# Folded norm sums, an activation scaled on ScalarE, and a layer norm joined with its modulation, in a two-block transformer kernel

## The reference, cut to what matters

```
# first block, end of each half (y: projected result, T x 1024)
x  = x + gate * rms_norm(y, g)              # after gla_out and after ffn_out
h2 = rms_norm(x, g') * (1 + scale) + shift  # input of ffn_in
# second block
h3 = x * (1 + scale_a) + shift_a            # input of qkv (no norm)
x  = layer_norm(ALPHA * x + gate_a * mix, ln1_g, ln1_b)
h4 = x * (1 + scale_f) + shift_f            # input of up
out = layer_norm(ALPHA * x + gate_f * down, ln2_g, ln2_b)
```

## Time and profile before

| | |
|---|---|
| median of 3 runs | 1060.26 us (1060.14 to 1066.72) |
| profiled execution | 1059.05 us, span 1057.3 us |
| PE busy | 980.9 us (93%) |
| DVE busy | 703.9 us (67%) |
| ACT busy | 551.0 us (52%) |
| norm sums on PE (line 614) | 112 instructions, 31.1 us |
| DMA | 196.79 MB, mean 186 GB/s |

### The profile page before, as it was taken

How to read it: one execution, slowest core, us unless ns; L and a number is a source line. 1 busy time by engine, 2 the same in 40 slices (tenths; PEclk the granted TensorE clock), 3 DMA queues, 4 the chain that set the end, 5 groups by cost and what they waited for, 6 DMA issues and landing times.

```text
span 1057.3 us, 19933 instructions
## 1 busy us (share of the span) xinstructions
PE 980.9 (93%) x8478; PEld 918.5 (87%) x8478; DVE 703.9 (67%) x1098; ACT 551.0 (52%) x830; POOL 27.2 (3%) x70
## 2 busy tenths in 40 slices
PE   5897999979999999699999999989999699999996
PEld 1477999869999999599898999888898699999995
DVE  2669937547777766598865543555668578888743
ACT  2658431555544443565745342656764466666433
POOL 2010000000000000130100000000000000000000
PEclk9898999999999999899999999999999989999999
DMA  9632765536888888247433436444357525555931
GB/s 329 234 121 80 264 234 187 181 127 212 278 275 283 281 274 309 72 149 252 153 120 102 149 113 169 140 160 132 110 201 228 208 99 184 189 188 188 331 100 40
DMA packets 57113, 196.79 MB, mean 186 GB/s; under 512 B 6064, under 2 KB 10560, under 8 KB 56768
## 3 DMA queue, kind: packets, MB, share of 16 engines
q1 hardware_dynamic: 51552, 187.72, 52.3%
q10 hardware_dynamic: 5216, 7.53, 2.6%
q0 software_dynamic: 256, 0.26, 0.1%
HBM read 194.43 MB, written 1.06 MB: 185 GB/s over the span
## 4 chain that ended last, share of the span: by engine, by line
PE 81%; DVE 9%; ACT 5%; DMA 3%; issue 1%; SPq 0%; ACTq 0%; DVEq 0%
PE panel_banks L401 67%; DMA raw<-in_panels 3%; PE work_banks L786 2%; DVE w_lo L1478 2%; PE work_banks L614 2%; ACT w_hi L969 1%; PE work_banks L573 1%; DVE raw L1511 1%; PE work_banks L715 1%; PE panel_banks L454 1%; PE work_banks L757 1%; PE work_banks L546 1%; PE work_banks L869 1%; PE work_banks L488 1%; PE work_banks L814 1%
## 5 line engine op out<-in xcount | busy, mean ns | idle before, releaser
L401 PE MATMUL panel_banks<-act_hi,w_hi 128*128 128x256 f32 (+1 forms) x1600 | 463.3, 290 | 26.3 <-DVE act_lo L1674 11.4
L401 PE MATMUL panel_banks<-act_lo,w_hi 128*128 128x256 f32 (+1 forms) x1600 | 454.5, 284 | 0.0
L401 PE MATMUL panel_banks<-act_hi,w_lo 128*128 128x256 f32 (+1 forms) x1600 | 453.9, 284 | 0.0
L1478 DVE TENSOR_TENSOR w_lo<-raw,w_hi 128x1024 fp32r<-128x1024 f32 x260 | 315.3, 1222 | 163.5 <-ACT w_hi L969 162.8
L969 ACT ACTIVATE w_hi<-raw 128x1024 fp32r<-128x1024 f32 x260 | 272.0, 1054 | 151.4 <-PE panel_banks L401 130.4
L401 PEld LDWEIGHTS panel_banks<-act_hi,w_hi 128*128 128x128 f32 x1600 | 304.6, 190 | 39.5 <-issue 19.5
L401 PEld LDWEIGHTS panel_banks<-act_lo,w_hi 128*128 128x128 f32 x1600 | 304.7, 190 | 1.8 <-issue 0.5
L401 PEld LDWEIGHTS panel_banks<-act_hi,w_lo 128*128 128x128 f32 x1600 | 304.4, 190 | 1.4
L401 PE MATMUL panel_banks<-hidden_hi,w_hi 128*128 128x256 f32 x352 | 98.0, 278 | 2.3 <-ACT hidden_hi L1186 2.3
L401 PE MATMUL panel_banks<-hidden_hi,w_lo 128*128 128x256 f32 x352 | 97.9, 278 | 0.0
L401 PE MATMUL panel_banks<-hidden_lo,w_hi 128*128 128x256 f32 x352 | 97.7, 278 | 0.0
(11 more groups left out here) (269 smaller groups left out, 1032.9 us busy)
## 6 DMA issues: line engine op xcount, KB each, us to landing
raw<-in_panels SPq DMA_DIRECT2D x356, 512.0 KB, 5.0
mix_work<-delta_rows ACTq DMA_DIRECT2D x2, 1024.0 KB, 11.8
x_t<-in_x ACTq DMA_DIRECT2D x1, 1024.0 KB, 9.4
gla_work<-in_ctx_x ACTq DMA_DIRECT2D x1, 1024.0 KB, 14.3
mix_work<-in_rel_bias ACTq DMA_DIRECT2D x1, 1024.0 KB, 10.0
out_x<-ffn_work SPq DMA_DIRECT2D x2, 512.0 KB, 2.6
mix_work<-in_rel_bias ACTq DMA_DIRECT2D x1, 768.0 KB, 14.3
c_wide<-in_c_rows ACTq DMA_DIRECT2D x1, 512.0 KB, 16.6
```

Of the source, the lines that this page charges most:

```text
L401: ins = pe.matmul(out_, a, b, start=start and p == 0, stop=stop and p == 2, skip_group_check=True)
L1478: dve.tensor_tensor(wlo[:, v_ % PARTS, :], raw[:, u % RAW, :], whi[:, v_ % PARTS, :].bitcast(F32), ALU.subtract)\
```

## The change: what it does

Five edits. (1) DVE adds the squares of two tiles (`fold`), so PE sums four tiles in place of eight, in the norm after `gla_out`, the one after `ffn_out`, and both variances; for the layer norm's mean DVE adds the two residual tiles into `sq2`. (2) After `ffn_out` ACT's last two weight copies, and DVE's subtractions for them, come behind the squares. (3) h3 is scaled on ACT instead of DVE. (4) The first layer norm's gain and bias are multiplied with the modulation on 128x8 columns, and h4 comes straight from `y3`; the plain result `xt` is made during turns 4 to 13 of the up projection, one tile a turn on DVE and then ACT. (5) The output is stored two tiles at a time.

```diff
-            for k in (0, 4):
+            for k in (0, 2, 4, 6):
...
-            def norm_part(name, count, r, src, bank=0, signal="norm_sum"):
+            def norm_part(name, count, r, src, bank=0, signal="norm_sum", tiles=1):
                 pe.wait_ge(S(name), count + r + 1)
-                for k in (2 * r, 2 * r + 1):
+                for k in range(2 * r, 2 * r + tiles):
...
             for i in range(11):          # ACT, ffn_out (DVE's loop likewise)
-                upper_parts(j + 2)
+                if i < 10:
+                    upper_parts(j + 2)
...
+            upper_parts(j + 1)           # ACT, after the four pairs
             act.wait_ge(S("norm_sum"), 4)
             factor(rs[:, 0:T], MB[:, 0, 0:T], D, 0, "norm_factor")
-            upper_tiles("h3_ready", lambda k: h3[:, k, :], "h3_hi")
+            for r in range(4):
+                act.wait_ge(S("x_new"), 5 + r)
+                for k in (2 * r, 2 * r + 1):
+                    act.activation(h3[:, k, :], xt[:, k, :], ACT.Identity, scale=..., bias=...)
+                for k in (2 * r, 2 * r + 1):
+                    act.wait_ge(S("h3_ready"), k + 1)
+                    act.activation(hhi[:, k, :], h3[:, k, :], ACT.Copy).then_inc(S("h3_hi"), 1)
...
+            def fold(wait_for, count, name):
+                dve.wait_ge(S(wait_for), count)
+                r = (count - 1) % 4
+                dve.tensor_tensor(sq2[:, 2 * r, :], sq2[:, 2 * r, :], sq2[:, 2 * r + 1, :], ALU.add).then_inc(S(name), 1)
+            for i in range(4):           # DVE, gla_out
+                fold("squares", i + 1, "folded")
+                if i < 3:
+                    lower_parts(j + 2)
+                j += 1
...
+            for r in range(4):           # DVE, after ffn_out
+                fold("squares", 9 + r, "folded")
+            lower_parts(j + 1)
+            for r in range(5):
+                if r < 4:
+                    normed(4, r)
+                    add_normed(r)
+                if r:
+                    for k in (2 * r - 2, 2 * r - 1):
+                        lower_tile(k, h3[:, k, :], "h3")
...
             def residual(turn, r):
-                dve.scalar_tensor_tensor(group(y3, r), group(xt, r), ALPHA, group(y3, r), ALU.mult, ALU.add)\
-                    .then_inc(S("ln_in"), 1)
+                then(dve.scalar_tensor_tensor(group(y3, r), group(xt, r), ALPHA, group(y3, r), ALU.mult, ALU.add))
+                dve.tensor_tensor(sq2[:, 2 * r, :], y3[:, 2 * r, :], y3[:, 2 * r + 1, :], ALU.add).then_inc(S("ln_in"), 1)
...
                 for r in range(4):       # DVE, layer_norm
                     dve.tensor_tensor(group(y3, r), group(y3, r), over_tiles(rs[:, 0:T], 2), ALU.subtract)
+                    if r >= 2:
+                        fold("ln_squares", 4 * count + r - 5, "folded")
+                for r in (2, 3):
+                    fold("ln_squares", 4 * count + r - 3, "folded")
...
+            dve.tensor_tensor(gcol[:], sc_a[:, 1, :], col("ln1_g_2", 0, 8), ALU.mult)
+            then(dve.tensor_tensor(sc_a[:, 0, :], sc_a[:, 1, :], col("ln1_b_2", 0, 8), ALU.mult))
+            then(dve.tensor_tensor(sc_a[:, 0, :], sc_a[:, 0, :], mod2[:, 24:32], ALU.add))
+            layer_norm(1)
+            staggered(lambda k: dve.scalar_tensor_tensor(h2[:, k, :], y3[:, k, :], gcol[:, k:k + 1], rs[:, T:2 * T],
+                                                         ALU.mult, ALU.mult).then_inc(S("ln_scaled"), 1),
+                      lambda k: lower_tile(k, h2[:, k, :], "h4", bias=sc_a[:, 0, k:k + 1]))
...
+                if 4 <= i < 4 + KT:      # DVE, in the up projection, before lower_parts
+                    dve.scalar_tensor_tensor(y3[:, i - 4, :], y3[:, i - 4, :], col("ln1_g_2", i - 4), rs[:, T:2 * T], ...)
...
+                if 6 <= i < 6 + KT:      # ACT, in the up projection, before the wait for up_done
+                    act.wait_ge(S("ln_scaled"), KT + i - 5)
+                    act.activation(xt[:, i - 6, :], y3[:, i - 6, :], ACT.Identity, bias=col("ln1_b_2", i - 6))
```

More of the change, by code:

```diff
@@ L299, in _ @@
                     .then_inc(S(f"landed{u % RAW}"), 16)
-            for k in (0, 4):
-                sp.wait_ge(S("out_ready"), k + 4)
-                sp.dma_start(out[:, k:k + 4], f_out[:, k:k + 4]).then_inc(S("out_stored"), 16)
-            sp.wait_ge(S("out_stored"), 32)
+            for k in (0, 2, 4, 6):
+                sp.wait_ge(S("out_ready"), k + 2)
+                sp.dma_start(out[:, k:k + 2], f_out[:, k:k + 2]).then_inc(S("out_stored"), 16)
+            sp.wait_ge(S("out_stored"), 64)
         @block.gpsimd
@@ L608, in _ @@
             gla_norm(3)
-            def norm_part(name, count, r, src, bank=0, signal="norm_sum"):
+            def norm_part(name, count, r, src, bank=0, signal="norm_sum", tiles=1):
                 pe.wait_ge(S(name), count + r + 1)
-                for k in (2 * r, 2 * r + 1):
+                for k in range(2 * r, 2 * r + tiles):
                     ins = pe.matmul(MB[:, bank, 0:T], ones[:, 0:P], src[:, k, :], start=(k == 0),
-                                    stop=(k == KT - 1))
+                                    stop=(k == 6 + tiles - 1))
                 if r == 3:
@@ L628, in _ @@
                 else:
-                    norm_part("squares", 0, n - 1, sq2)
-            norm_part("squares", 0, 3, sq2)
+                    norm_part("folded", 0, n - 1, sq2)
+            norm_part("folded", 0, 3, sq2)
             for r in range(4):
@@ L634, in _ @@
                     pe.wait_ge(S("norm_factor"), 2)
-                norm_part("squares", 4, r, sq2)
+                norm_part("squares", 4, r, sq2, tiles=2)
             for i in range(22):
@@ L687, in _ @@
             for r in range(4):
-                norm_part("squares", 8, r, sq2)
+                norm_part("folded", 4, r, sq2)
             for i in range(12):
@@ L1217, in _ @@
                 ins.then_inc(S("panel_evacuated"), 1)
+            upper_parts(j + 1)
             act.wait_ge(S("norm_sum"), 4)
             factor(rs[:, 0:T], MB[:, 0, 0:T], D, 0, "norm_factor")
-            upper_tiles("h3_ready", lambda k: h3[:, k, :], "h3_hi")
+            for r in range(4):
+                act.wait_ge(S("x_new"), 5 + r)
+                for k in (2 * r, 2 * r + 1):
+                    act.activation(h3[:, k, :], xt[:, k, :], ACT.Identity, scale=sc_a[:, 1, k:k + 1], bias=mod2[:, k:k + 1])\
+                        .then_inc(S("h3_ready"), 1)
+                for k in (2 * r, 2 * r + 1):
+                    act.wait_ge(S("h3_ready"), k + 1)
+                    act.activation(hhi[:, k, :], h3[:, k, :], ACT.Copy).then_inc(S("h3_hi"), 1)
             def delta_rows():
@@ L1405, in _, with layer_norm @@
                 j += 1
[L1407 removed]
+            def layer_norm(count):
                 act.wait_ge(S("ln_sum"), count)
@@ L1415, in layer_norm @@
                 factor(rs[:, T:2 * T], MB[:, 1, 0:T], D, 1, "ln_factor")
[L1416 to L1429, removed]
+            layer_norm(1)
+            upper_tiles("ln_scaled", lambda k: h2[:, k, :], "h4_hi", bias=lambda k: sc_a[:, 0, k:k + 1])
             for i in range(22):
@@ L1440, in _ @@
                     hidden_upper(i - 1, "hidden2_gated")
+                if 6 <= i < 6 + KT:
+                    act.wait_ge(S("ln_scaled"), KT + i - 5)
+                    act.activation(xt[:, i - 6, :], y3[:, i - 6, :], ACT.Identity, bias=col("ln1_b_2", i - 6))\
+                        .then_inc(S("x3_ready"), 1)
                 act.wait_ge(S("up_done"), i + 1)
@@ L1457, in _ @@
                 ins.then_inc(S("panel_evacuated"), 1)
-            layer_norm(2, "ln2_b_2", f_out, "out_ready")
+            layer_norm(2)
+            for k in range(KT):
+                act.wait_ge(S("ln_scaled"), 2 * KT + k + 1)
+                act.activation(f_out[:, k, :], y3[:, k, :], ACT.Identity, bias=col("ln2_b_2", k)).then_inc(S("out_ready"), 1)
         @block.vector
@@ L1699, in _ @@
             j = 12
-            for i in range(3):
-                lower_parts(j + 2)
+            def fold(wait_for, count, name):
[6 more added lines that the diff above has]
+                    lower_parts(j + 2)
                 j += 1
-            j += 1
             def group(v, r):
@@ L2010, in _, with layer_norm @@
                 j += 1
-            def layer_norm(count, gain, after=None):
+            def layer_norm(count):
                 dve.wait_ge(S("ln_in"), 4 * count)
@@ L2079, in _ @@
                 j += 1
+            dve.wait_ge(S("x3_ready"), KT)
             for r in range(4):
                 residual(first["down"][1], r)
-            layer_norm(2, "ln2_g_2")
+            layer_norm(2)
+            for k in range(KT):
+                dve.scalar_tensor_tensor(y3[:, k, :], y3[:, k, :], col("ln2_g_2", k), rs[:, T:2 * T], ALU.mult, ALU.mult)\
+                    .then_inc(S("ln_scaled"), 1)
```

17 lines of the change are left out of this document (8 added, 9 removed).

## The result

The changed kernel takes 1054.2 us in the median of 6 runs (1052.78 to 1057.14). The kernel before, run beside it, takes 1065.38 us in the median of 6 (1060.14 to 1067.54), where the first three had given 1060.26. The ratio is 0.9907 (95% interval 0.9882 to 0.9932): 0.9% faster, some 10 us. The forecast was a ratio of 0.9893 (11.3 us) and a time of 1048.9 us; the ratio lies in the interval, the time misses by 5.3 us and lies outside the range.

What follows compares the result with a forecast made beforehand. PE's products, 81% of the chain of waits, bound the kernel except where norms make PE wait. Terms -1.0 - 6.1 - 3.2 - 1.0 gave -11.3 us: 1047.75 from the profiled 1059.05, plus 1.2 for the median, 1048.9; range 1045.3 to 1053.3.

Steps and rivals of the forecast that it cites:

- After gla_out: Norm after gla_out: folding turns two blocks of four sums into pairs, -0.86 us, and shortens the last sum, -0.1; together -1.0.
- The squares after ffn_out: After ffn_out: squares ahead of the last two weight copies let DVE's multiply begin at 430.25 instead of 433.99, -3.7 us.
- h3: After ffn_out: with scaling on ACT, DVE's multiply to the first qkv result takes 11.5 us instead of 13.9, -2.4.
- Ahead of the first mean: First layer norm before its variance: DVE's residual add and three column operations delay the mean's subtraction, +1.05 us.
- First variance: First layer norm: mean subtraction to PE's last sum takes 5.6 us instead of 6.8, -1.2, bounds -0.7 and -2.0.
- h4: First layer norm: first scaling to first up result takes about 10.2 us instead of 13.2, -3.1, bounds -1.5 and -3.5.
- Plain result in up: Up projection: the added DVE and ACT operations fit in idle time and cost nothing; without that idle, 3.2 us.
- Second layer norm: Last norm: sum of y3 takes 2.8 us instead of 3.47, -0.65; variance between -0.35 and +1.0, taken as 0.
- Output: End of the kernel: a smaller last transfer and an earlier issue save 0.35 us, bounds nothing and 0.8.
- where it was 8.5: Sign after ffn_out: DVE's multiply starts about 4.8 us after PE's last product, where it was 8.5.
- shifts as a block: Between the four norm places: PE-bound work only moves in time, so the estimate sums what each place gains.
- the rival of a clock that takes part of it back: Half clock lasting through both variances, h3 and h4: up to 4.5 us less gain, 1053.4 us; chance 0.31.

Runs made afterwards that it cites:

- second pair: Traces of the kernel before and the changed kernel, each run again unaltered; ratios to the kernel before 0.9988 and 0.9924, the changed kernel's median 1056.4 us.

## Why the prediction was right or wrong

- **After gla_out**, -1.0: -0.8 in the first pair of traces. The second pair shows +1.1, where the clock was 0.75 from 202 to 206 us, as gla_out began; that stretch lies ahead of the first fold. From the first sum to the factor the changed kernel took 14.0 us in both, the kernel before 14.9 and, with two panels at 113 ns, 14.5.
- **The squares after ffn_out**, -3.7: -3.5 and -4.4 measured, 3.8 with the order put back. Right, with the same new wait (copies, then subtractions) as forecast.
- **h3**, -2.4: -1.7 in both pairs. The mechanism was right. The size was off because ACT's two scaled tiles take 1.09 us, not 0.84, and since PE took up its products at the half clock.
- **Ahead of the first mean**, +1.05: +0.94, from the last residual's start to the subtraction 4.23 us in both traces instead of 3.29 (fold 0.42, and 0.48 from the first added column operation to the subtraction).
- **First variance**, -1.2: -0.65. This is the term that the clock mis-sized: all eight sums at half clock.
- **h4**, -3.1: -2.75 and -2.5.
- **Plain result in up**, 0: 0.
- **Second layer norm**, sum -0.65: -0.65. Variance, taken as 0 between -0.35 and +1.0: +1.0. The pause of 2.8 us was where the forecast saw the danger; it took the middle, and the poor end came, in all six traces with folds and an unfilled pause there (5.8 to 6.2 us).
- **Output**, -0.35: -0.2. A transfer lands nearly as late for half the bytes, 2.5 us against 2.6; the 0.6 us that the prediction estimated from the Trainium skill's formula (DMA: Bandwidth & Descriptors, section on the anatomy of one DMA, for another kind of queue) is not there. The page's row of the changed kernel:

```profile
out_x<-ffn_work SPq DMA_DIRECT2D x4, 256.0 KB, 2.5
```

PE's last product of ffn_out was read as 425.5; it ended at 425.86, so "where it was 8.5" should be 8.1. In the chances, 0.40, 0.12 and a tenth of 0.31 make 0.55, not 0.56.

The step that failed for the time is the last of the sum, "the median of the runs is 1.2 above it, so 1048.9". The level it started from was low: the profiled execution had 113 ns in ffn_out, worth 2.4 us, and an early start, and two of the three runs were at 1060.1 and 1060.3, where the medians of larger sets are 1064.6 and 1065.1. With 1064.6 the same sum gives 1053.3, against 1054.2 and 1056.4 measured. The range held no term for that; that everything between the places "shifts as a block" was wrong by up to 4.5 us a stretch. The second failure is smaller, the clock: the rival of a clock that takes part of it back came true by 2.6 to 2.9 us of its 4.5 (last variance 1.0, h3 0.7, first variance 0.55, h4 0.35 and 0.6), though part of h3's is ACT's longer tiles. It was worth being the forecast: the earlier trace rows had already shown both pauses at the lower level. The Trainium skill (TensorE: Matmul & The Clock Gate, section on HAM oscillation) gives the same advice, to keep PE's work together, and these traces agree: 0.51 and 0.50 against 1.00 with PE kept busy.

That the ratio came out so near (0.9907 for 0.9893) is in part luck. The places give 7.7 us in the two pairs of traces, and the spans of these pairs differ by 5.9 and 6.8 us; the second measurement of the changed kernel gave 0.9924, some 8 us.

## What to carry to other kernels

A pause of PE costs twice, once as idle time and once as the half clock behind it; thinning PE's work in such a pause buys less than its count of instructions, and filling the pauses with products that nobody reads gave some 5 us, in the trace and in the medians, on the changed kernel; on the kernel before, filled less fully, it gave nothing that the times show. Look for what stands ahead of a chain in an engine's own queue: two weight copies moved behind the squares were worth some 4 us, the largest part of the change, and two subtractions and five column operations another 1.8. Before a sum is set against three runs, ask how far executions of the same kernel differ; here it was as much as the change.

## What was not expected of the hardware

Back-to-back three-pass products of 256 columns start 113 or 118 ns apart at the same granted clock of 1.00, with one pace held through a whole stretch and changing only behind a pause of PE, in the same kernel (179 and 172 products in 20 us). No view showed a cause. The start of the program to the first gla factor varies too, 198.5 to 203.0 us over the traces.
